# Conformer convolution: from four phases with two chunks on VectorE to eight phases with all chunks on TensorE

## The chip, the cores and the metric

One core of a Trainium2 chip. The metric is device microseconds of one launch, as the median of three runs.

## The reference

Two decoder layers on 512 tokens of 1024 channels, in float32. Each layer is a half-step SwiGLU feed-forward, a token mixer and a second half-step feed-forward, each between RMS norms and added to the residual. The mixer of layer 0 is sliding-window attention; that of layer 1 is the convolution module that the change is about:

```
a = h @ w_pw1 + b_pw1                       # 512 x 2048
u = a[:, :1024] * sigmoid(a[:, 1024:])
y = causal depthwise conv of u, width 31, one filter per channel, + b_dw
y = silu(layer_norm over the 1024 channels (y))
out = y @ w_pw2 + b_pw2
```

## The kernel before

Activations lie transposed, channels on the 128 partitions and 512 tokens along the row, so 1024 channels are 8 chunks. All dense products run on TensorE as three products each (high part by high part, high by low, low by high; L401 to L403). The weights come as one stream of slots of 128 x 1024 floats. SyncE loads slot n into a ring of four (`load`, L286), ScalarE copies its high part (L971) once TensorE has finished slot n - 4, VectorE subtracts to get the low part (`next_slot`, L1259), and TensorE multiplies it (`body`). VectorE takes the result from PSUM with the RMS factor (`scale_to`, L1292).

The first pointwise layer has 16 slots, two for each chunk: the value and the gate. When both are scaled, ScalarE takes the sigmoid (L1196) and VectorE makes u (`gate`, L1547 or L1553).

The depthwise convolution is done in two ways. Chunks 0 and 1 (`NAT = 2`) are done on VectorE, one tap at a time, each a multiply and add over 128 x 512 (`taps`, L1604 and L1608), spread by hand between the other instructions of the loop over chunks. The other six (`CONVS = 6`) are done on TensorE. The tokens of a chunk are put in `PH = 4` phases, token n*4 + q into phase q. u goes to DRAM and comes back with (channel, phase) on the partitions, 32 channels x 4 phases for each of 4 groups (`store_u` L306, `load_groups` L312). In that layout the 31 taps become `SHIFTS = 9` banded matrices per group, made on the host. One chunk is 2 pairs of groups x 9 shifts x 4 tiles of 64 x 64 = 72 matmuls of 128 columns in float32 (`convolve`, L857). The matrices, 2 of 576 KB a chunk, lie in five places (`MATS = 5`) and are loaded by SyncE (L302).

The norm over channels needs a mean over all of them. A mean over four early chunks is taken first (`sum_early`, L877) and subtracted from all; what is left of the mean and the sum of squares are added up by TensorE (L868, L891), and two broadcasts bring them to all partitions (`broadcast_phases`, L937). z goes through DRAM to the layout of channels again (L316, L320), is normalised (L1683, L1686), and the second pointwise layer starts (`four_slots`, L468 to L472).

All engines run orders written out by hand, tied by semaphores. TensorE's in this stage is: slots 4 and 5, slot 6, then for each of the first four chunks two slots and `convolve`, slot 15, the early mean, chunk 4 in two halves with the spread of the mean between them (L930), chunk 5 in two halves with sums between. VectorE's last split (slot 15) stands before its last gate.

Of the kernel before, what the change touches and what calls it, by code (L numbers as in the profile page):

```python
# [54 lines left out]
PH = 4  # L55
# [8 lines left out]
NAT = 2  # L64
CONVS = KD - NAT
EARLY = 4
# [32 lines left out]
def build_program(nc, stream, xT, cols_in, rope_c, rope_s, ident_in, ident_b_in, mask_in, mats_in, conv_in,  # L99
                  u_dram, z_dram, outT):  # L100
    ctx = ExitStack()
    with ctx:
# [3 lines left out]
        def sem(name):  # L106
# [37 lines left out]
        ug = al[:, 0:2 * GROUPS * (PAD + NT)].rearrange("p (i g n) -> p i g n", i=2, g=GROUPS)  # L144
        conv_c = sb("conv_consts", [P, P + CONVS * GROUPS + NAT * (CW + 1)])
        same_q, b_dw = conv_c[:, 0:P], conv_c[:, P:P + CONVS * GROUPS]
        at = P + CONVS * GROUPS
        w_nat = [[conv_c[:, at + c * CW + i:at + c * CW + i + 1] for i in range(CW)] for c in range(NAT)]
        at += NAT * CW
        b_nat = [conv_c[:, at + c:at + c + 1] for c in range(NAT)]  # L150
        at += NAT

        extra = sb("tap_matrix", [P, SHIFTS * P])
        spare = extra[:, 0:2 * T]
        swapped = [*(a_lo[:, k, :].bitcast(F32) for k in range(KD)), spare[:, 0:T], spare[:, T:2 * T]]
        MAT = 2 * SHIFTS * HALF
        extra2 = sb("tap_matrix2", [P, MAT])
        mats = [*(fv[:, i * MAT:(i + 1) * MAT] for i in range(3)), extra[:, :], extra2[:, :]]
        MATS = len(mats)

        kf = kT[:, :, :].rearrange("p a n -> p (a n)")
        zg = [z.rearrange("p (g n) -> p g n", g=GROUPS) for z in
              (kf[:, 0:T], kf[:, T:2 * T], rc[:, :], rs[:, :], U[:, 1, :], G[:, 1, :])]
        zsq_sum, *zsq = [z.rearrange("p (g n) -> p g n", g=GROUPS) for z in (G[:, 0, :], U[:, 0, :], ss[:, :])]
        m0 = sb("mean_early", [P, NT])
        dl, dl_sq, var = sb("mean_rest", [P, PH]), sb("mean_rest_sq", [P, PH]), sb("var", [P, PH])
        std = var
        early = sq[:, 0, :].rearrange("p (j n) -> p j n", j=EARLY)
        y = qT
        yv = y[:, :, :].rearrange("p a n -> p (a n)")  # L170
        u_nat = [yv[:, NAT * T + c * (CW - 1 + T):NAT * T + (c + 1) * (CW - 1 + T)] for c in range(NAT)]
        nat_acc = [y[:, KD - NAT + c, :] for c in range(NAT)]
        nat_sq, nat_sum = nat_acc, sq[:, 1, :]
# [6 lines left out]
        conv_out = [two_banks[i] for i in (3, 2, 3, 2, 3, 0)]  # L180
# [54 lines left out]
        s_ug = [sem(f"u_groups_loaded{i}") for i in range(2)]  # L235
# [5 lines left out]
        s_tap, s_m0bc, s_nat = sem("tap_added"), sem("early_mean_broadcast"), sem("direct_chunk_centred")  # L241
        s_nsq, s_nsum = sem("direct_chunk_squared"), sem("direct_chunks_added")
# [28 lines left out]
        def _(sp):  # L271
# [26 lines left out]
            def load_matrices(i):  # L298
                for k in range(MATS + PAIRS * (i - 1) if i else 0, min(MATS + PAIRS * i, PAIRS * CONVS)):
                    if i:  # L300
                        sp.wait_ge(s_cv, k - MATS + 1)
                    sp.dma_start(mats[k % MATS], mats_in[k // PAIRS, k % PAIRS, :, :]).then_inc(s_mats[k % MATS], 16)  # L302

            def store_u(i):
                sp.wait_ge(s_u, NAT + i + 1)
                sp.dma_start(u_dram[i, :, :], u[i % 2]).then_inc(s_ud[i % 2], 16)  # L306

            def load_groups(i):
                sp.wait_ge(s_ud[i % 2], 16 * (i // 2 + 1))
                if i >= 2:  # L310
                    sp.wait_ge(s_cv, PAIRS * (i - 1))
                sp.dma_start(ug[:, i % 2, :, PAD:], by_groups(u_dram, i)).then_inc(s_ug[i % 2], 16)  # L312
# [5 lines left out]
            def load_y(i):  # L318
                sp.wait_ge(s_zd[i % 4], 16 * (i // 4 + 1))
                sp.dma_start(y[:, NAT + i, :], z_dram[i, :, :]).then_inc(s_y[NAT + i], 16)  # L320
# [18 lines left out]
            sp.wait_ge(s_nat, NAT)  # L339
            for i in range(EARLY):  # L340
                load_y(i)
            store_z(4)
            sp.wait_ge(s_sqmm, 1)
            load_y(4)
            store_z(5)
            load_y(5)
            loads(conv_turn + PW1_SLOTS // RING, SLOTS // RING)
# [12 lines left out]
        def _(pool):  # L360
# [28 lines left out]
            for i in range(2):  # L389
                nc.gpsimd.memset(ug[:, i, :, 0:PAD], 0.0).then_inc(s_zeros, 1)  # L390
            for c in range(NAT):
                nc.gpsimd.memset(u_nat[c][:, 0:CW - 1], 0.0).then_inc(s_zeros, 1)
# [5 lines left out]
        def _(pe):  # L398
# [436 lines left out]
            def convolution(n0, sub):  # L835


                def convolve(j, halves=range(PAIRS)):

                    if 0 in halves:  # L840
                        pe.wait_ge(s_ug[j % 2], 16 * (j // 2 + 1))
                        if j == 0:
                            pe.wait_ge(s_zeros, 4)
                        if j == 1:
                            pe.wait_ge(s_rpre, sub + 1)
                        if j >= 2:
                            pe.wait_ge(s_zg, j - 1)
                        if j == CONVS - 1:
                            pe.wait_ge(s_evac, n0 + 14)
                    for i in halves:  # L850
                        k = PAIRS * j + i
                        pe.wait_ge(s_mats[k % MATS], 16 * (k // MATS + 1))
                        for m in range(SHIFTS):
                            for odd, rows, out in ((0, 0, 0), (0, 1, 1), (1, 0, 1), (1, 1, 0)):
# [4 lines left out]
                                                        ug[at, j % 2, 2 * i + odd, m:m + NT],  # L859
# [3 lines left out]
                def sum_groups(out, src, first, last):  # L863

                    for g in range(GROUPS):
                        for part in range(2):
                            to = slice(part * HALF, (part + 1) * HALF)
                            ins = nc.tensor.matmul(out[to, 0:PH], src[:, g, to], same_q[:, 0:PH],  # L868
                                                   start=(first and g == 0), stop=(last and g == GROUPS - 1),
                                                   skip_group_check=True)  # L870
                    return ins

                def sum_early():
                    pe.wait_ge(s_zg, EARLY)
# [6 lines left out]
                def sum_rest(j):  # L881
                    pe.wait_ge(s_zc, j + 1)
                    sum_groups(BCAST, zg[j], False, j == CONVS - 1).then_inc(s_dlmm, 1)

                def sum_direct(out, src, ready, first):

                    pe.wait_ge(s_nsum, ready)
                    for q in range(PH):
                        for part in range(2):
                            to = slice(part * HALF, (part + 1) * HALF)  # L890
                            ins = nc.tensor.matmul(out[to, q:q + 1], src[:, q * NT + to.start:q * NT + to.stop],  # L891
                                                   ones[:, 0:1], start=(first and q == 0), stop=False,
                                                   skip_group_check=True)
                    return ins

                def sum_squares(added):
                    if added:
                        pe.wait_ge(s_root, 3 * sub + 1)
                        sum_direct(STAT, nat_sq[0], 2, True)
                        pe.wait_ge(s_zsqadd, CONVS - 2)  # L900
                        sum_groups(STAT, zsq_sum, False, False)
                        return
                    pe.wait_ge(s_zsq, CONVS)
                    sum_groups(STAT, zsq[(CONVS - 1) % 2], False, True).then_inc(s_sqmm, 1)
# [22 lines left out]
            def spread_phases(out, v):  # L927

                for q in range(PH):
                    ins = nc.tensor.matmul(out[:, q * NT:(q + 1) * NT], ident[:, q:q + 1].broadcast_to([P, P]),  # L930
                                           v[:, :], start=True, stop=True)
                return ins

            def broadcast_phases(out, v):

                for q in range(PH):
                    ins = nc.tensor.matmul(out[:, q * NT:(q + 1) * NT], v[:, q:q + 1].broadcast_to([P, P]),  # L937
# [920 lines left out]
```

## Time and profile before

| | |
|---|---|
| median of three runs | 1828.2 us (1825.47 to 1830.34) |
| profiled execution | 1828.89 us, span 1827.1 us |
| TensorE busy in the span | 1808.8 us, 99% |
| VectorE busy in the span | 1020.5 us, 56% |
| slots 6 to 15 of the first pointwise layer and the convolution, to the first product of the second | 1304.1 to 1404.97 us |

The span is the time between the first and the last instruction of the profiled execution. A busy TensorE is one that has products in flight; they overlap, so the lengths of single products don't add up to a time, and the distances of their starts do.

### The profile page before, as it was taken

How to read it: one execution, taken by the hardware profiler on the slowest of the kernel's cores; microseconds unless marked ns; L12 is line 12 of the kernel's file. 1: busy time of each engine (PE TensorE's matmuls, PEld its weight loads, DVE VectorE, ACT ScalarE, POOL GpSimd, SP SyncE). 2: the span in 40 equal slices, each digit the busy share in tenths (PEclk: the TensorE clock that was granted, in tenths of full speed). 3: DMA queues.
4: the chain of work that ended last, by engine and by line, in shares of the span. 5: the costliest groups of instructions: out<-in, count | busy, mean ns of one | idle time of the engine just before them, and what ended most of it. 6: DMA issues, size and time to landing. Idle time of an engine off the chain costs nothing.

```text
span 1827.1 us, 26277 instructions
## 1 busy us (share of the span) xinstructions
PE 1808.8 (99%) x9934; PEld 1508.4 (83%) x9941; DVE 1020.5 (56%) x1484; ACT 644.1 (35%) x977; POOL 31.2 (2%) x60
## 2 busy tenths in 40 slices
PE   9999999999999999999999999999998999999999
PEld 7888888887698888888888888888887988888887
DVE  6534434589767434434774344347898774344345
ACT  5322313455744223222442232224414542222223
POOL 1000000022000000000000000000000000000000
PEclk9999999999999999999999999999998999999999
DMA  6333333422032333333333333333544333333331
GB/s 205 116 96 102 92 101 92 119 86 79 10 96 93 102 93 92 104 92 102 106 94 102 92 92 104 93 103 104 180 162 138 93 94 102 92 92 104 93 102 58
DMA packets 64078, 186.09 MB, mean 102 GB/s; under 512 B 7264, under 2 KB 19168, under 8 KB 64000
## 3 DMA queue, kind: packets, MB, share of 16 engines
q1 hardware_dynamic: 61824, 182.69, 32.7%
q0 software_dynamic: 1600, 1.52, 0.3%
q8 instruction: 55, 0.90, 0.2%
q10 hardware_dynamic: 576, 0.79, 0.1%
q14 instruction: 23, 0.19, 0.0%
HBM read 179.08 MB, written 5.24 MB: 101 GB/s over the span
## 4 chain that ended last, share of the span: by engine, by line
PE 92%; DVE 5%; issue 1%; ACT 1%; DMA 0%; ACTq 0%; SPq 0%; DVEq 0%
PE bank L401 27%; PE bank L402 27%; PE bank L403 27%; PE bank L494 4%; DVE qT L1608 2%; PE bank L499 2%; DVE w_lo L1259 1%; PE bank L762 1%; PE bank L794 1%; PE bank L738 1%; PE bank L428 1%; PE bank L777 0%; PE bank L420 0%; PE bank L857 0%; PE bank L441 0%
## 5 line engine op out<-in xcount | busy, mean ns | idle before, releaser
L1259 DVE TENSOR_TENSOR w_lo<-w_raw,w_hi 128x1024 fp32r<-128x1024 f32 x302 | 369.2, 1225 | 417.2 <-ACT w_hi L971 406.6
L401 PE MATMUL bank<-x_hi,w_hi 128*128 128x512 f32 x1432 | 558.9, 390 | 0.0
L402 PE MATMUL bank<-x_lo,w_hi 128*128 128x512 f32 x1432 | 557.2, 389 | 0.0
L403 PE MATMUL bank<-x_hi,w_lo 128*128 128x512 f32 x1432 | 557.2, 389 | 0.0
L971 ACT ACTIVATE w_hi<-w_raw 128x1024 fp32r<-128x1024 f32 x302 | 317.1, 1054 | 559.9 <-PE bank L403 547.4
L401 PE MATMUL bank<-a_hi,w_hi 128*128 128x512 f32 (+1 forms) x894 | 331.5, 371 | 1.1 <-issue 1.1
L402 PE MATMUL bank<-a_lo,w_hi 128*128 128x512 f32 (+1 forms) x894 | 329.6, 369 | 0.0
L403 PE MATMUL bank<-a_hi,w_lo 128*128 128x512 f32 (+1 forms) x894 | 329.5, 369 | 0.0
L403 PEld LDWEIGHTS bank<-x_hi,w_lo 128*128 128x128 f32 x1432 | 268.8, 188 | 56.3
L401 PEld LDWEIGHTS bank<-x_hi,w_hi 128*128 128x128 f32 x1432 | 268.8, 188 | 56.2 <-issue 0.7
L402 PEld LDWEIGHTS bank<-x_lo,w_hi 128*128 128x128 f32 x1432 | 268.8, 188 | 55.2
L401 PEld LDWEIGHTS bank<-a_hi,w_hi 128*128 128x128 f32 x894 | 168.4, 188 | 30.9 <-issue 1.6
L403 PEld LDWEIGHTS bank<-a_hi,w_lo 128*128 128x128 f32 x894 | 168.4, 188 | 28.2
L402 PEld LDWEIGHTS bank<-a_lo,w_hi 128*128 128x128 f32 x894 | 168.5, 188 | 28.1
L1292 DVE TENSOR_TENSOR up_tmp<-bank,r_pre 128x512 f32<-128x512 f32 x96 | 66.2, 690 | 183.7 <-PE bank L403 182.3
L1009 ACT ACTIVATE a_hi<-up_tmp 128x512 f32 (+1 forms) x88 | 55.6, 632 | 267.2 <-DVE up_tmp L1302 267.2
L1007 ACT ACTIVATE gate_tmp<-gate_tmp 128x512 f32<-128x512 f32 x88 | 55.7, 632 | 158.3 <-DVE gate_tmp L1292 158.2
L1304 DVE TENSOR_TENSOR a_lo<-up_tmp,a_hi 128x512 f32 (+1 forms) x88 | 60.9, 692 | 79.9 <-ACT a_hi L1009 79.9
L1292 DVE TENSOR_TENSOR gate_tmp<-bank,r_pre 128x512 f32<-128x512 f32 x106 | 72.3, 683 | 7.1 <-ACT r_pre L995 6.9
L1302 DVE TENSOR_TENSOR up_tmp<-up_tmp,gate_tmp 128x512 f32<-128x512 f32 x88 | 60.9, 692 | 13.7 <-ACT gate_tmp L1007 3.3
L980 ACT ACTIVATE x_hi<-h_resid,cols 128x256 fp32r<-128x256 f32 (+1 forms) x88 | 46.5, 528 | 44.3 <-DVE h_resid L1378 41.6
L1314 DVE TENSOR_TENSOR f_out<-bank,f_out 128x512 f32 (+2 forms) x73 | 45.0, 620 | 25.1 <-PE bank L403 25.0
(206 smaller groups left out, 1322.1 us busy)
## 6 DMA issues: line engine op xcount, KB each, us to landing
w_raw<-stream SPq DMA_DIRECT2D x312, 512.0 KB, 3.6
f_out<-mats_in SPq DMA_DIRECT2D x8, 576.0 KB, 5.6
tap_matrix<-mats_in SPq DMA_DIRECT2D x4, 576.0 KB, 7.3
h_resid<-xT SPq DMA_DIRECT2D x8, 256.0 KB, 6.0
qT<-stream SPq DMA_DIRECT2D x8, 256.0 KB, 6.2
u_scratch<-V SPq DMA_DIRECT2D x6, 256.0 KB, 2.2
a_lo<-u_scratch SPq DMA_DIRECT2D x6, 256.0 KB, 2.7
qT<-z_scratch SPq DMA_DIRECT2D x6, 256.0 KB, 3.6
```

The source lines that it names most:

```text
L401: nc.tensor.matmul(out, lw[0], lx[0], start=first, stop=False)
L402: nc.tensor.matmul(out, lw[0], lx[1], start=False, stop=False)
L403: return nc.tensor.matmul(out, lw[1], lx[0], start=False, stop=last)
L494: nc.tensor.matmul(bank[FIRST_BANKS[s]][:, tok], w[KD * s + k][part], x_hi[:, k, tok], start=(k == 0 and tok == A and part == 0), stop=Fal ...
L971: nc.scalar.activation(w_hi[:, s, :], raw[:, s, :], ACT.Copy).then_inc(s_hi, 1)
L980: nc.scalar.activation(x_hi[:, k, tok], h[:, k, tok], ACT.Copy, scale=col("pre", sub * KD + k)).then_inc(done, 1)
L1007: nc.scalar.activation(g, g, ACT.Silu).then_inc(s_act, 1)
L1009: nc.scalar.activation(a_hi[:, chunk, :], U[:, (s // 2) % 2, :], ACT.Copy).then_inc(s_ahi, 1)
L1259: nc.vector.tensor_tensor(w_lo[:, s, :], raw[:, s, :], w_hi[:, s, :].bitcast(F32), ALU.subtract).then_inc(s_lo, 1)
L1292: nc.vector.tensor_tensor(dst, out[:, :], r_pre[:, :], ALU.mult).then_inc(s_evac, 1)
L1302: nc.vector.tensor_tensor(U[:, p, :], U[:, p, :], G[:, p, :], ALU.mult).then_inc(s_prod, 1)
L1304: nc.vector.tensor_tensor(a_lo[:, chunk, :], U[:, p, :], a_hi[:, chunk, :].bitcast(F32), ALU.subtract).then_inc(s_a, 1)
```

## The change

The convolution runs in eight phases. A chunk then has 8 groups of 16 channels x 8 phases of 64 tokens, 5 shifts, and 4 pairs x 5 shifts x 4 tiles = 80 matmuls of 64 columns. All eight chunks go this way, and the taps on VectorE with all that belongs to them are gone. The matrices are 4 of 320 KB a chunk, in 14 places: eight are loaded by SyncE ahead of the slots of the third feed-forward block, six after it, and the other 18 by ScalarE, in sets, as places come free. u of seven chunks has room at once. The early mean is over three chunks. The last gate stands ahead of the last split of a weight slot, z of the last chunk is stored last, and statistics and broadcasts have eight phases on 64 partitions.

```diff
-PH = 4
+PH = 8
-NAT = 2
-CONVS = KD - NAT
-EARLY = 4
+CONVS = KD
+EARLY = 3
...
             conv_turn = (PW1 + 2 * RING) // RING
-            loads(2, conv_turn)
+            loads(2, FFN2 // RING + 1)
+            first_matrices(FREE_MATS)
+            loads(FFN2 // RING + 1, conv_turn)
             for j in range(KD):
                 n = PW1 + 2 * RING + 2 * j
                 load(n, n % RING)
-                if j >= RING:
-                    load_matrices(j - RING + 1)
-                load(n + 1, (n + 1) % RING)
+                if j < KD - 1:
+                    load(n + 1, (n + 1) % RING)
                 if j == 0:
                     sp.wait_ge(s_root, 3 * 4 + 1)
-                    load_matrices(0)
-                if j >= NAT:
-                    store_u(j - NAT)
-                    load_groups(j - NAT)
-            load_matrices(CONVS - 1)
-            for i in range(EARLY):
+                    first_matrices(F_MATS)
+                store_u(j)
+                load_groups(j)
+            load(n + 1, (n + 1) % RING)
+            for i in range(EARLY + 1):
                 store_z(i)
...
                 first_body(n0, sub)
-                body(n0 + 6, 2)
                 for i in range(EARLY):
-                    for n in range(2 * i + 7, 2 * i + 9):
+                    for n in range(2 * i + 6, 2 * i + 8):
                         body(n0 + n, n % RING)
                     convolve(i)
-                body(n0 + 15, 3)
+                body(n0 + 12, 0)
                 sum_early()
-                convolve(4, range(0, 1))
+                body(n0 + 13, 1)
+                convolve(EARLY)
+                for n in range(14, 16):
+                    body(n0 + n, n % RING)
+                for i in range(EARLY + 1, CONVS - 1):
+                    convolve(i)
                 pe.wait_ge(s_m0, 1)
-                spread_phases(BCAST, m0).then_inc(s_m0bc, 1)
-                convolve(4, range(1, 2))
-                convolve(5, range(0, 1))
-                pe.wait_ge(s_nat, NAT)
-                sum_direct(BCAST, nat_sum, 1, True).then_inc(s_dlmm, 1)
-                sum_rest(4)
-                convolve(5, range(1, 2))
-                sum_squares(True)
-                sum_rest(5)
-                sum_squares(False)
+                pe.wait_ge(s_rest, 2)
+                sum_groups(BCAST, rest, True, False)
+                convolve(CONVS - 1)
+                sum_centred(6)
+                pe.wait_ge(s_root, 3 * sub + 1)
+                pe.wait_ge(s_zsqadd, CONVS - 2)
+                sum_groups(STAT, zsq_sum, True, False)
+                sum_centred(7).then_inc(s_dlmm, 1)
+                pe.wait_ge(s_zsq, CONVS)
+                sum_groups(STAT, zsq[(CONVS - 1) % 2], False, True).then_inc(s_sqmm, 1)
...
+                def load_matrices(i, count=PAIRS):
+                    for k in range(MATS + PAIRS * i, MATS + PAIRS * i + count):
+                        act.wait_ge(s_cv, k - MATS + 1)
+                        act.dma_start(mats[k % MATS], mats_in[k // PAIRS, k % PAIRS, :, :]
+                                      ).then_inc(s_mats[k % MATS], 16)
...
                         scale_to((U, G)[e][:, j % 2, :], bank[FIRST_BANKS[n - n0] if n < n0 + RING else n % RING], n, 5)
+                        if (j, e) == (KD - 2, 0):
+                            dve.wait_ge(s_m0mm, 1)
...
                     gate(j)
-                    if 2 <= j < KD - 1:
-                        k = taps(k, 3 if j == 2 else 4)
+                    if EARLY <= j < 2 * EARLY:
+                        biased(j - EARLY)
+                        add_early(j - EARLY)
+                next_slot(n, n % RING)
                 centred(4)
```

## Rows read from the trace of the kernel before

**Rows 1.** The page: busy time of engines, and the span in 40 slices.
```profile
PE 1808.8 (99%) x9934; PEld 1508.4 (83%) x9941; DVE 1020.5 (56%) x1484; ACT 644.1 (35%) x977; POOL 31.2 (2%) x60
...
PEclk9999999999999999999999999999998999999999
```

**Rows 2.** The chain of waits at the convolution's end: start us, us, what.
```profile
1375.22 3.97 DVE qT L1608 x6
...
1384.56 2.88 DMA u_scratch<-V
...
1387.46 2.92 DMA a_lo<-u_scratch
...
1404.97 0.50 PE bank L468
```

**Rows 3.** TensorE's timeline in that stage: start us, us, line, output<-inputs, count, idle before.
```profile
1299.23 0.39 PE L401 MATMUL bank<-x_hi,w_hi 128*128 128x512 f32 x1
...
1318.95 0.39 PE L401 MATMUL bank<-x_hi,w_hi 128*128 128x512 f32 x1
...
1320.40 4.16 PE L857 MATMUL bank<-a_lo,f_out 64*64 64x128 f32 x144
...
1335.64 2.20 PE L857 MATMUL bank<-a_lo,f_out 64*64 64x128 f32 x72
...
1379.85 1.89 PE L877 MATMUL bank<-sq_tmp,conv_consts 128*128 128x128 f32 x8 [3.85 <-DVE rope_sin L1583]
1381.66 3.24 PE L857 MATMUL bank<-a_lo,tap_matrix 64*64 64x128 f32 x72
...
1390.42 3.86 PE L857 MATMUL bank<-a_lo,f_out 64*64 64x128 f32 x72 [2.30 <-DMA a_lo<-u_scratch]
...
1399.55 1.16 PE L937 MATMUL bank<-ident,mean_rest 128*128 128x128 f32 x8
1400.71 1.91 PE L937 MATMUL bank<-ident,var 128*128 128x128 f32 x8
```

**Rows 4.** Stretches: busy us and instructions of PE, PEld, DVE, ACT, POOL; granted clock; DMA share; GB/s.
```profile
1380.40:1383.85 3.45, 3.45 (x46) 2.98 (x48) 2.66 (x4) 1.19 (x2) 0.00 (x0) 0.51 0.25 52
1390.69:1394.10 3.41, 3.41 (x72) 3.25 (x64) 3.20 (x6) 1.26 (x2) 0.00 (x0) 0.50 1.07 330
...
1397.44:1404.97 7.53, 7.14 (x86) 5.34 (x87) 4.20 (x11) 3.91 (x7) 0.00 (x0) 0.77 0.37 100
```

**Rows 5.** VectorE's groups from 1304.1 to 1405: count, busy us, mean ns, idle before.
```profile
L1608 DVE SCALAR_TENSOR_TENSOR qT<-qT,conv_consts 128x512 f32<-128x512 f32 x60 | 40.5, 744 | 0.0
L1259 DVE TENSOR_TENSOR w_lo<-w_raw,w_hi 128x1024 fp32r<-128x1024 f32 x12 | 14.6, 1216 | 0.2 <-ACT w_hi L971 0.2
L1553 DVE SCALAR_TENSOR_TENSOR V<-up_tmp,cols,gate_tmp 128x512 f32<-128x512 f32 x6 | 6.9, 1156 | 4.7 <-ACT gate_tmp L1196 4.7
...
L1292 DVE TENSOR_TENSOR gate_tmp<-bank,r_pre 128x512 f32<-128x512 f32 x6 | 4.1, 681 | 0.0
L1640 DVE TENSOR_REDUCE sq_tmp<-kT 128x128 f32<-128x512 f32 x2 | 2.2, 1076 | 0.1
...
L1583 DVE TENSOR_TENSOR kT<-bank,conv_consts 128x512 f32<-128x512 f32 x2 | 1.4, 688 | 0.0
```

**Rows 6.** Products in flight on TensorE in two short stretches of chunk 0's convolution.
```profile
1320.60:1320.65 0.05, 0.05 (x8) 1.00 0.23 82
1320.66:1320.71 0.05, 0.05 (x12) 1.00 0.60 246
```

**Rows 7.** TensorE's timeline: small sums on two tiles, and the attention's transposes.
```profile
492.95 0.71 PE L777 MATMUL bank<-ident,f_out 64*128 64x64 f32 x16
...
1398.99 0.64 PE L868 MATMUL bank<-conv_consts,sum_sq 128*64 128x4 f32 x16
```

**Rows 8.** The DMA view, 1290 to 1404: count, KB each, median us to landing.
```profile
tap_matrix<-mats_in SPq DMA_DIRECT2D x4, 576.0 KB, 7.3
```

**Rows 9.** SyncE's queue: the weight loads of slots 10 to 13.
```profile
1297.16 11.12 SPq L286 DMA_DIRECT2D w_raw<-stream  x4
```

More of the change, by code:

```diff
@@ L148, in build_program @@
[L148 to L154, printed above, removed]
+        spare = sb("spare", [P, 2 * T])[:, :]
         swapped = [*(a_lo[:, k, :].bitcast(F32) for k in range(KD)), spare[:, 0:T], spare[:, T:2 * T]]
         MAT = 2 * SHIFTS * HALF
-        extra2 = sb("tap_matrix2", [P, MAT])
@@ L158, in build_program @@
-        mats = [*(fv[:, i * MAT:(i + 1) * MAT] for i in range(3)), extra[:, :], extra2[:, :]]
-        MATS = len(mats)
+        more = sb("tap_matrices", [P, 2 * MAT])[:, :]
         kf = kT[:, :, :].rearrange("p a n -> p (a n)")
+        y = qT
+        yv = y[:, :, :].rearrange("p a n -> p (a n)")
+        Y_MATS = 5
         zg = [z.rearrange("p (g n) -> p g n", g=GROUPS) for z in
-              (kf[:, 0:T], kf[:, T:2 * T], rc[:, :], rs[:, :], U[:, 1, :], G[:, 1, :])]
+              (kf[:, 0:T], kf[:, T:2 * T], rc[:, :], rs[:, :], yv[:, Y_MATS * MAT:Y_MATS * MAT + T],
+               U[:, 1, :], u[0], G[:, 1, :])]
@@ L171, in build_program @@
-        u_nat = [yv[:, NAT * T + c * (CW - 1 + T):NAT * T + (c + 1) * (CW - 1 + T)] for c in range(NAT)]
-        nat_acc = [y[:, KD - NAT + c, :] for c in range(NAT)]
-        nat_sq, nat_sum = nat_acc, sq[:, 1, :]
+        early = sq[:, 0, :].rearrange("p (j n) -> p j n", n=NT)
+        rest = sq[:, 1, :].rearrange("p (g n) -> p g n", g=GROUPS)
+        mats = [room[:, i * MAT:(i + 1) * MAT]
+                for room, first, count in ((spare, 0, 1), (more, 0, 2), (fv, 0, 1), (yv, 0, Y_MATS), (fv, 1, 5))
+                for i in range(first, first + count)]
@@ L174, in build_program @@
+        MATS = len(mats)
+        F_MATS = 3, 9, 10, 11, 12, 13
+        FREE_MATS = [i for i in range(MATS) if i not in F_MATS]
         first_raw = qT[:, :, :].rearrange("p a n -> p (a n)").rearrange("p (s n) -> p s n", s=RING)
@@ L234, in build_program @@
         s_ud = [sem(f"u_in_dram{i}") for i in range(2)]
-        s_ug = [sem(f"u_groups_loaded{i}") for i in range(2)]
+        s_ug = [sem(f"u_groups_loaded{i}") for i in range(CONVS)]
         s_zd = [sem(f"z_in_dram{i}") for i in range(4)]
@@ L296, in by_groups, with first_matrices @@
                 return dram[j, :, :].rearrange("(g c) (q n) -> (c q) g n", g=GROUPS, q=PH)
[L298 to L302, printed above, removed]
+            def first_matrices(which):
+                for k in which:
+                    sp.dma_start(mats[k], mats_in[k // PAIRS, k % PAIRS, :, :]).then_inc(s_mats[k], 16)
             def store_u(i):
-                sp.wait_ge(s_u, NAT + i + 1)
+                sp.wait_ge(s_u, i + 1)
                 sp.dma_start(u_dram[i, :, :], u[i % 2]).then_inc(s_ud[i % 2], 16)
@@ L865, in sum_groups, with sum_centred @@
                     for g in range(GROUPS):
[L866 to L870, printed above, removed]
-                    return ins
+                        ins = nc.tensor.matmul(out[0:NT, 0:PH], src[:, g, :], same_q[:, 0:PH],
+                                               start=(first and g == 0), stop=(last and g == GROUPS - 1),
+                                               skip_group_check=True)
+                    return ins
+                def sum_centred(j):
+                    pe.wait_ge(s_zc, j + 1)
+                    return sum_groups(BCAST, zg[j], False, j == CONVS - 1)
                 def sum_early():
-                    pe.wait_ge(s_zg, EARLY)
+                    pe.wait_ge(s_rpre, sub + 1)
                     for j in range(EARLY):
@@ L879, in sum_early @@
                     last.then_inc(s_m0mm, 1)
[L881 to L894, printed above, removed]
@@ L1843 @@
     b_groups = np.broadcast_to(b_dw[0][order].reshape(KD * GROUPS, GC, 1), (KD * GROUPS, GC, PH)).reshape(KD * GROUPS, P).T
-    direct = (*(w_dw.reshape(CW, D)[:, c * P:(c + 1) * P].T for c in range(NAT)), cols(b_dw[0])[:, :NAT])
     bf = ml_dtypes.bfloat16
```

212 lines of the change are left out of this document (89 added, 123 removed).

## The prediction

> **What bounds the kernel now.** I read the page first. TensorE is busy through nearly the whole span, at full clock in all slices but one, so only work or waits of TensorE inside the convolution can move the time; the one slice at 0.8 of the clock lies there [rows 1]. The chain of waits over that stretch says what sets the pace at its end: VectorE with its taps (L1608), then the gate, then two transfers, then TensorE again from 1390.42 [rows 2]. So for the changed stretch I take TensorE's own timeline [rows 3] and VectorE's groups [rows 5], and split TensorE's 100.9 us between the start of slot 6 and the first product of the second pointwise layer.
>
> A slot of the first pointwise layer is 8 blocks of 0.680 us (29 blocks between 1299.23 and 1318.95), 5.44 us; slot 6 starts three slots ahead of the first convolution, at 1320.40 - 16.3 = 1304.1. From one convolution to the next it is 15.24 us [rows 3]: two slots (10.88) and a chunk of 4.36. A chunk is 144 products (72 matmuls, each recorded as two); less the length of the last one they start 27.2 ns apart ((4.16 - 0.27) / 143), 3.92 us, and 0.44 is spent at the turns from one kind of product to the other. Ten slots (54.4) and four chunks (17.4) bring TensorE to 1375.9. Then it waits 3.9 us for VectorE's z of chunk 3; sums the early mean (1.8); convolves chunk 4 in halves, the first in 3.2, with a spread of the mean between them; waits 2.3 for the last u to come back from DRAM; and takes 7.0 for chunk 5 with sums between its halves, to 1397.44. The first product of the next layer starts 7.53 us later. The two halves that take 3.2 and 3.8 instead of 2.1 lie in stretches with the clock at 0.50 to 0.51, the lower level of 1.2 GHz, behind the 3.9 us of idling [rows 4].
>
> **The change, part by part.** *Taps off VectorE.* 62 instructions go, 60 of which are 40.5 us; with them go six operations on the direct chunks. In their place come two more z (0.69 each), three additions and small ones [rows 5]. In the steady part VectorE then has two splits, two scalings, a wait for the sigmoid, a gate, a bias and a reduction for each two slots: 2 x 1.22 + 2 x 0.68 + 4.7 / 6 + 1.16 + 0.69 + 1.08 = 7.5 us beside at least 13 us on TensorE. So it is never late there: each z is ready some 10 us before the next convolution wants its banks, and the 3.9 us wait, the clock loss behind it and the spread go.
>
> *All chunks on TensorE, eight phases.* A chunk becomes 4 pairs x 5 shifts x 4 tiles = 80 matmuls, 160 products, of 64 columns instead of 128, and there are eight chunks. All depends on what a product of 64x64 weights and 64 columns costs, which no row shows. In the conv of now four products start within 0.06 us (8 in flight from 1320.60 to 1320.65, 12 from 1320.66 to 1320.71) [rows 6]: four tiles run side by side, each with a new product every 4 x 27.2 = 109 ns, that is 0.85 ns for each of 128 columns. 64 columns would be 54 ns. The smallest products of the trace, 64 columns of weights and 1 or 4 moving ones on two tiles, start (0.64 - 0.20) / 15 = 29.3 ns apart [rows 7], 58.6 ns for each tile, which is then about what a load of 64 columns costs a tile. If that 58.6 belongs to the tile, four tiles give 14.7 ns a product and a chunk costs 2.34 us. If instead 27 to 29 ns belongs to the stream of instructions, whatever the tile, a chunk costs 4.35 to 4.7. The transposes, on two tiles as well, show 32.6 ns ((0.71 - 0.22) / 15) [rows 7]. I take the tile's reading, because four starts within 0.06 us speak against a spacing by instruction, and because the conv of now gets the same 27 ns from four tiles at 109 that the small sums get from two at 58.6. Bounds: 13.3 (columns alone) and 32.6 ns.
>
> The Trainium skill has a rule against this: TensorE: Matmul & The Clock Gate, section Back-to-back issue gap, gives 1 to 64 columns the same gap of about 60 cycles, a floor of some 25 ns from start to start. By that rule a chunk would cost 4.0 us, and eight such chunks more than the six of now. The Trainium skill's page TensorEngine Tiling (Array Packing), section Tiling Modes, says on the other hand that different tiles execute weight loads and matmuls in parallel; that part the trace bears out with its four starts within 0.06 us.
>
> *TensorE up to slot 15.* Ten slots 54.4, four chunks at 2.34 + 0.44 = 11.1, early mean 0.7 (six products instead of eight, at full clock): 66.2, so slot 15 ends at 1370.3, where it now ends at 1375.9. Chunks 4 to 6 follow without a slot between: 0.2 + 7.0, and the sum of the rest 0.5, to 1378.0.
>
> *Last gate ahead of the last split.* Now a split stands before the gate. Scaling of the last slot (0.68), the wait for its sigmoid (4.7 / 6), gate (1.16), the way to DRAM (2.88) and back (2.92) are 8.4 us with 0.1 for the steps between, 8.5 [rows 2, 5]. With scaling at 1370.5 the last chunk can begin at 1379.0. The groups are read in runs of 256 B instead of 512 B, for which no row exists; I add 0.5 (bounds 0 and, at twice the 2.92, 2.9). So chunk 7 starts at 1379.5, 1.5 us after TensorE is free. This chain of transfers, not TensorE, is what is late next, and it is all that is left of the old waits. It ends at 1381.9.
>
> *Tap matrices on ScalarE's queue.* 32 matrices of 320 KB replace 12 of 576 KB: 3.3 MB more. Eight go out before the third feed-forward block's first slots, six at its end, 18 from ScalarE. At the boundary the weight ring has slack: a slot's load stands some 20 us ahead of its split, and 2.6 MB at the 330 GB/s that a stretch here shows [rows 4] take 8 us. In the conv ScalarE issues each set of four after a split, for places free since the convolution before, and is busy for 35% of the span [rows 1]. The last two go out at about 1373.5; 576 KB ones took 7.3 us to land [rows 8], so they land by 1380.8 at worst, where the third pair starts at 1380.7. Nothing, or 0.5 us.
>
> *SyncE's queue.* The first weight load of the stretch is now queued behind the first u and its reading back: 1303.4 instead of 1297.16 [rows 9]. It lands at 1307 and is wanted after slot 6, at 1309.5: nothing. z of chunk 7 is stored last and read back by about 1391; its channel is normalised eighth, some 13 us after the first. Nothing.
>
> *The tail.* The same steps from the last convolution on, 7.53 us [rows 2, 3], but each broadcast of eight phases is 16 products with 128 columns of weights instead of 8, at up to 0.124 ((1.16 - 0.29) / 7). The mean's starts at 1399.55 and then ends at 1401.4, the deviation's 1.9 later, at 1403.3 instead of 1402.6 [rows 3]: +0.7. The clock may fall again in the 1.5 us gap or in the tail; today's tail has it at 0.77 [rows 4]. I give 0.3 for it, with 0 and 3 as bounds.
>
> Sum: 1381.9 + 0.3 + 7.53 + 0.7 = 1390.4, against 1404.97: 14.6 us less. From there on nothing changes. The profiled execution took 1828.9 us around a span of 1827.1, 0.7 over the median of the three runs; 1828.9 - 14.6 - 0.7 = 1813.6, so 1814.
>
> **Rivals.** *The floor belongs to the instructions (27.2 ns).* Slot 15 ends at 1304.1 + 54.4 + 4 x 4.79 + 0.7 = 1378.4, the last four chunks take 18.1, to 1396.5, and the tail 8.2: 1404.7, 0.3 us less than now. The waits are gone and the eight chunks have eaten them. At the 29.3 ns of the small sums it is 2.7 us more. Time 1828 to 1831, no change. For it: no run of products in these rows averages less than 27.2 ns. This is what the rule of the Trainium skill quoted above amounts to; with its own 25 ns the time would be 1825.
>
> *In between, 20 ns*, if loads of four tiles partly share a port: chunks of 3.2. Slot 15 at 1373.8, last chunk to 1387.2, tail to 1395.4: 9.5 less, 1819.
>
> *Slower.* The 64x64 products keep to the transposes' 32.6 ns [rows 7]: 1280 products x 5.4 ns = 6.9 more than at 27.2, so 6.6 slower, 1835. It decides from 31.7 ns on. Against it: those have twice the columns of weights.
>
> **Chances.** Tile's floor 0.66, between 0.07, instruction's floor 0.21, slower 0.06. 0.3% of this kernel is 5.5 us, about what a measurement of it can tell from no change. The first two are faster, 0.73; same 0.21; slower 0.06. The likeliest case alone has 1810 to 1819: 13.3 ns and no loss of clock at the lower end (two to three less), slow pieces in the transfers and a low clock at the upper. The whole range goes from 1810 to 1829 and leaves out the upper half of the instruction's floor and the slower case.
>
> **What would show it.** The convolution's line with 1280 products; a run of 160 in about 2.5 us (4.4 if I am wrong); from one convolution to the next about 13.7 us instead of 15.24; no wait of TensorE for VectorE before the early mean; a wait of 1 to 2 us for the transfer of u before the last chunk; VectorE's L1608 gone and its share down from 56%; the full clock up to slot 15. If the period stays near 15.7, the floor was the instruction's and the prediction is wrong there. If the period is right and the end isn't, look at the matrices from ScalarE's queue and at the 256 B runs.

## The result and the profile after

The changed kernel takes 1833.3 us (median of 8 runs, 1831.9 to 1838.4) where the one before takes 1828.0 on the same chip (8 runs): ratio 1.0032, 95% interval 1.0023 to 1.0042. It is 5.3 us slower by the medians. I had forecast 1814, within 1810 to 1829.

The page of the profiled execution (1832.03 us, span 1830.2), to set beside [rows 1]:

```profile
PE 1810.6 (99%) x10347; PEld 1510.9 (83%) x10347; DVE 982.8 (54%) x1425; ACT 643.8 (35%) x977; POOL 31.1 (2%) x63
...
PEclk9999999999999999999999999999997999999999
...
q8 instruction: 58, 0.95, 0.2%
```

VectorE lost its taps, as the change says. The slice of the convolution has a clock of 0.7 instead of 0.8. The last line I had passed over in both pages: a queue of its own brings instructions, 0.95 MB in 58 transfers, that is 16 KB each.

TensorE's timeline answers to [rows 3] (start us, us, line, output<-inputs, count, idle before):

```profile
1327.47 2.56 PE L856 MATMUL bank<-a_lo,qT 64*64 64x64 f32 x160
1341.07 0.81 PE L856 MATMUL bank<-a_lo,qT 64*64 64x64 f32 x40
1341.70 1.91 PE L856 MATMUL bank<-a_lo,f_out 64*64 64x64 f32 x114
1345.00 0.34 PE L856 MATMUL bank<-a_lo,f_out 64*64 64x64 f32 x6 [1.40 <-issue]
1350.85 0.78 PE L878 MATMUL bank<-sq_tmp,conv_consts 128*128 128x64 f32 x6
```

A whole chunk is 160 products in 2.56 us; less the length of the last, 0.22, they start 14.7 ns apart, as forecast. From the first convolution (1313.87) to the second and third it is 13.6 us. The early mean no longer waits for VectorE. But chunk 2 stops after 154 products (40 + 114) for 1.40 us, and the row names no releaser but "issue": nothing that the profile knows held TensorE.

The chain of waits from there on answers to [rows 2] (start us, us, what):

```profile
1370.74 3.66 PE bank L856 x240
1374.40 1.84 issue
1376.24 2.09 PE bank L856 x124
1378.34 1.75 issue
1380.09 1.86 PE bank L856 x112
1381.95 0.97 PE bank L865 x15
1382.92 3.25 issue
1386.18 0.17 PE bank L865
1386.35 3.37 PE bank L856 x127
1389.71 1.39 issue
1391.10 0.73 PE bank L856 x33
1391.84 6.20 PE bank L865 x64
1398.04 7.02 PE bank L910 x32
```

The last gate and the transfers of the last u are not in this chain at all; [rows 2] had them. The products run out three times ahead of the last chunk and once inside it. Count them between two stops: 124 in the chain (the timeline has all 128 there), then 112 + 15 = 127, then 1 + 127 = 128. Each product goes with one weight load (the page has 10347 of either), so each stop comes after about 256 instructions, and 16 KB for 256 instructions are 64 bytes each. The Trainium skill's page Advanced Engine Details and Errata, section ISA Cache, has the same size: a line of 16 KB holds 256 instructions, and there are only two lines (it also gives TensorE's cache as 128 KB, which would hold more). The trace agrees with the 256; how many lines there are no run here settles, and the page has no price for a line. The DMA view puts the transfer of such a piece ahead of the end of a stop. Of three stretches of the third stop, 1382.92 to 1383.88, to 1384.85 and to 1386.20, it is in the second (queue, transfers, MB, share of time):

```profile
q1 hardware_dynamic: 935, 0.24, 106.5%
q8 instruction: 1, 0.02, 6.0%
```

TensorE goes on 1.3 us after it. The same holds for the other four stops of this trace: each ends 1.4 to 1.7 us after a piece has moved. From one restart to the next a piece takes 3.85, 6.09 and 4.92 us, and 128 products at 14.7 ns use one up in 1.9.

Stretches with the granted clock answer to [rows 4] (us; busy us and instructions of PE, PEld, DVE, ACT, POOL; clock; DMA share; GB/s):

```profile
1370.74:1374.40 3.66, 3.66 (x241) 3.56 (x241) 2.87 (x4) 2.83 (x3) 0.00 (x0) 1.00 0.93 333
...
1385.85:1389.26 3.41, 3.08 (x113) 2.98 (x115) 0.00 (x0) 0.00 (x0) 0.00 (x0) 0.50 0.93 245
...
1392.67:1407.41 14.74, 14.74 (x90) 12.91 (x88) 3.51 (x10) 3.91 (x7) 0.00 (x0) 0.50 0.40 110
```

Behind the stops the clock is at its lower level, 1.2 GHz, for 3.4 us and then for the 14.7 us up to the first product of the next layer (and 2.3 us beyond it, 17.1 in all). From the start of slot 6 (1302.99) to that product (1407.41) it is 104.4 us; before it was 100.9, and I had forecast 86.3.

### The profile page after: what moved, and what is told of

It is laid out like the page before. It is cut to its first block, busy times and chain, and to the rows that moved or that the text cites. A ratio compares the mean times of both kernels' runs of the same rounds, so it can differ in the third digit from the quotient of the medians.

```text
span 1830.2 us, 27076 instructions
## 1 busy us (share of the span) xinstructions
PE 1810.6 (99%) x10347; PEld 1510.9 (83%) x10347; DVE 982.8 (54%) x1425; ACT 643.8 (35%) x977; POOL 31.1 (2%) x63
## 4 chain that ended last, share of the span: by engine, by line
PE 97%; DVE 1%; issue 1%; ACT 0%; ACTq 0%
PE bank L397 28%; PE bank L399 28%; PE bank L398 28%; PE bank L490 4%; PE bank L495 2%; PE bank L856 1%; PE bank L790 1%; PE bank L734 1%; PE bank L758 1%; PE bank L424 1%; PE bank L416 0%; PE bank L773 0%; PE bank L865 0%; PE bank L910 0%; PE bank L437 0%
## 5 line engine op out<-in xcount | busy, mean ns | idle before, releaser
L1278 DVE TENSOR_TENSOR gate_tmp<-bank,r_pre 128x512 f32<-128x512 f32 x106 | 72.4, 684 | 7.1 <-ACT r_pre L968 6.9
```

The costliest lines, as they stand in the source:

```text
L1278: nc.vector.tensor_tensor(dst, out[:, :], r_pre[:, :], ALU.mult).then_inc(s_evac, 1)
```

## The experiments

The theories: **F**, TensorE outruns the supply of its instructions wherever many cheap products stand in a row. **U**, the late last chunk is due to the transfers around the last u and z. **C**, a TensorE that idles falls to the lower clock, and that makes the last chunk, the small sums and the broadcasts dear. All kernels are edits of the changed one. "Stage" is the time from the first product of the convolution to the first product of the next layer in the profiled execution: 93.5 us in the changed kernel. In the kernel before, counted from the same point, 10.9 us after the start of slot 6, it is 90.0, of which 10.2 at the lower clock. "Last chunk begins after" counts from the first product of the convolution, and "lower clock" is the time at 1.2 GHz within the stage, both in us of the profiled execution. Each ratio is to the kernel before on the same chip, with a 95% interval, from 4 to 12 runs of a version.

| kernel | median us | ratio to before, interval | stage | last chunk begins after | lower clock |
|---|---|---|---|---|---|
| the change | 1833.3 | 1.0032, 1.0023 to 1.0042 | 93.5 | 72.4 | 18.2 |
| double_mid | 1834.9 | 1.0045, 1.0028 to 1.0062 | 95.8 | 77.2 | 18.9 |
| double_late | 1837.0 | 1.0052, 1.0035 to 1.0069 | 97.5 | 79.5 | 17.8 |
| few_shifts | 1826.9 | 0.9996, 0.9986 to 1.0006 | 88.6 | 67.2 | 20.9 |
| early_z | 1834.1 | 1.0032, 1.0019 to 1.0044 | 95.7 | 73.6 | 23.2 |
| no_mats | 1831.9 | 1.0019, 1.0009 to 1.0030 | 93.1 | 70.5 | 21.4 |
| filled | 1833.7 | 1.0031, 1.0020 to 1.0043 | 91.9 | 73.5 | 16.6 |
| interleave | 1829.5 | 1.0009, 0.9999 to 1.0018 | 96.3 | 73.9 | 24.5 |
| interleave_warm | 1827.6 | 1.0000, 0.9990 to 1.0009 | 89.4 | 72.9 | 10.1 |
| few_warm | 1829.0 | 1.0008, 0.9998 to 1.0018 | 90.3 | 75.2 | 15.0 |
| inter_short | 1830.5 | 1.0018, 1.0009 to 1.0027 | 93.1 | 69.7 | 17.6 |
| inter_tail | 1832.4 | 1.0023, 1.0011 to 1.0034 | 98.9 | 72.0 | 25.7 |
| warm_tail | 1828.5 | 1.0003, 0.9994 to 1.0012 | 93.1 | 71.2 | 16.6 |

A profile is one execution, and these kernels spread more than the one before: interleave from 1825.4 to 1834.9 (its profiled execution took 1834.9), inter_tail from 1825.5 to 1837.2 (profiled: 1837.2). So the medians decide on times, and the profiles on what happens in which order.

**A chunk's products twice.** In the middle (chunk 1), and at the end (chunk 5).

```diff
-                        for m in range(SHIFTS):
+                        for m in (*range(SHIFTS), *range(SHIFTS if j == 5 else 0)):
```

> The products of chunk 1, which lie between slots 9 and 10, are issued twice (320 instead of 160; the result is the same). Theory F (TensorE outruns the supply of its own instructions: in the changed kernel's trace it idles four times at the end of the convolution, 1.4 to 3.3 us, each time 128 products, that is 256 instructions, after the last, and each idling ends 1.4 to 1.7 us after a 16 KB instruction transfer): 128 products between slots are supplied ahead while a slot runs, so most of the extra ones cost 14.7 ns, 2.4 us, and at most one idling of 1.5 us is added: 5.8 + 2.4 to 3.9, ratio to the kernel before 1.0045 to 1.0055. Theory U (the end of the convolution waits for the last u and its DRAM trip, and the rest is the lower clock): slot 15 ends 2.4 us later and everything with it, 1.0045.

> The products of chunk 5, which follow chunk 4 with no slot between, are issued twice (same result). Theory F: each 128 products there take the 3.85 to 6.1 us from one idling to the next and not 1.9, so 160 more take 4.8 to 7.6 us, and there is one more idling: ratio 1.006 to 1.0075. Theory U: TensorE only waits there for the last u, which lands at about 1380.4, 5.9 us before the last chunk begins, so 2.4 us more are hidden: ratio 1.003 as without them.

double_mid: 236 products in 3.65 us, a stop of 1.73, then 84 more, in the middle of the layer, with the same "issue" as the releaser. double_late, the chain of waits:

```profile
1371.38 3.66 PE bank L856 x240
1375.04 1.84 issue
1376.88 2.09 PE bank L856 x125
1378.97 1.63 issue
1380.61 2.10 PE bank L856 x125
1382.70 3.45 issue
1386.15 2.09 PE bank L856 x128
1388.25 3.55 issue
```

The reader is to see the counts: 240, and then one stop for every 128 products, whatever chunk they belong to. 160 products more moved the last chunk by 7.0 us (79.5 - 72.4), not by 2.3. That is F, and no wait for data gives this pattern.

The times say less. double_late costs 3.7 us against the change, less than the 4.8 to 7.6 that F had: in its profile the stage is only 4.0 longer, since the last chunk, late as it is, runs without a stop. double_mid costs 1.6, and the intervals of the two overlap, so that late products are dearer than early ones is shown by the traces and not by the times.

**Fewer products.** Leaves out three of five shifts in chunks 4 to 6.

```diff
-                        for m in range(SHIFTS):
+                        for m in ((0, PAD) if j in (4, 5, 6) else range(SHIFTS)):
```

> Leaves out three of the five shifts of chunks 4, 5 and 6: 64 products each instead of 160, 288 fewer in all. Theory F: two idlings less before the last chunk; it starts when the last u has landed, at about 1381 instead of 1386.3, at full clock, and the tail goes back from 15.6 us towards 8.2 to 10: 10 to 13 us less than the changed kernel, ratio to before 0.996 to 0.998. Theory U: what sets the start of the last chunk is not TensorE's own work, so it starts within 0.5 us of 1386.3 and the ratio stays at 1.003.

```profile
1373.33 4.51 DMA u_scratch<-V
...
1377.85 2.85 DMA a_lo<-u_scratch
...
1380.74 4.32 PE bank L856 x159
1385.06 1.55 issue
1386.62 0.27 PE bank L856
1386.88 5.89 PE bank L865 x64
1392.77 7.02 PE bank L910 x32
```

Now the transfers of the last u are in the chain, as the prediction had them, and the last chunk begins at 1380.74, 5.3 us earlier than in the change. U falls: it had the last chunk where it was. For F this run alone says little, since 288 products fewer are 4.2 us less work even at 14.7 ns. And the clock did not recover as I had expected: TensorE idled 4.3 us for VectorE's last z, ran at half clock from 1377.8, and the tail kept its 13 us (5.89 + 7.02). So the supply is only a part of the loss.

**z of chunks 0 to 2 stored ahead of the last u.**

```diff
+                if j == KD - 1:
+                    for i in range(EARLY):
+                        store_z(i)
                 store_u(j)
...
-            for i in range(EARLY + 1):
-                store_z(i)
+            store_z(EARLY)
```

> The stores of z of chunks 0 to 2 stand ahead of the last u's store on SyncE's queue (they are centred by 1356) instead of behind its reading back. Theory F with contention (the third idling, 3.25 us, is long because the 16 KB of instructions stand behind z stores in pieces of 256 B): it shrinks to 1.5 to 2, 1 to 3 us less than the changed kernel, ratio 1.0015 to 1.0025. If instructions have their way free of other transfers: 1.003, and the third idling stays over 3 us.

The third stop stayed (3.25 us), and the time is that of the change. This does not clear the transfers of z, though. With its stores out of the way, SyncE issues the reading back of z earlier, from 1382.48, and between the restart at 1382.28 and the piece at 1385.94 the DMA engines still move 282 GB/s. What the piece waits behind stays open here.

**No late matrices.** Leaves out the loads of the last six tap matrices and TensorE's waits for them (not shown in the cut).

```diff
-                        if e == 0 and j >= RING:
+                        if e == 0 and RING <= j < KD - 1:
                             load_matrices(j - RING)
...
-                load_matrices(KD - RING, PAIRS * CONVS - MATS - PAIRS * (KD - RING))
```

> Leaves out the loads of the last six tap matrices (2 MB between 1366 and 1378), so chunks 6 and 7 use older ones. Theory F with contention (the third piece of 256 instructions came late, 3.8 us instead of 1.05 after TensorE resumed, because the DMA engines were full of matrices and z): the idlings of 1.84, 1.75 and 3.25 us shrink, the third to under 2, the last chunk starts 2 us earlier, 1831. If the supply has its own pace, nothing moves: 1833.

The stops are 0.89, 1.48 and 1.61 us instead of 1.84, 1.75 and 3.25, and the last chunk begins 1.9 us earlier, as F with contention said; inside the last chunk one of 2.38 us gives part of it back (the change has 1.39 there). In the traces data traffic stretches the supply, and without these loads TensorE still stops; the median is 1.4 us lower, which the intervals can't tell from no change. Note two things more. The store of the last u took 2.0 us here (issued 1374.71, read back from 1376.73) and 3.8 in the change (1373.50, 1377.30). And the clock fell at 1385.9 as in the change, though none of these three stops was longer than 1.61.

**Work that fills the stops.** Four products of 512 columns behind chunk 4 and behind chunk 5.

```diff
                 for i in range(EARLY + 1, CONVS - 1):
                     convolve(i)
+                    if i < 6:
+                        keep_warm(4, out=4)
```

> The changed kernel with four products of 512 columns (0.85 us, eight instructions) added after chunk 4 and again after chunk 5, into a free bank; nothing is left out. It has 1.7 us more work in the stretch that sets the end. Theory F (TensorE's idlings there are waits for instructions, 3.85 us or more a piece of 256 whatever it computes): the added products fill idling time, the idlings of 1.84, 1.75 and 3.25 us shrink by about what is added, and the last chunk starts within 0.5 us of where it did (72.4 us after the first convolution): 1833, perhaps 1 less where the clock stays up. If the idlings are something else (a wait for a bank or for data), all comes 1.7 us later: 1835.

1.7 us of work more cost 0.4 us by the medians, less than the measurement can tell. In the profiled execution, the fastest of six (1829.35), the stops ahead of the small sum are 1.08 and 0.39 us instead of 1.84 and 1.75, but the third was still 3.05, and the last chunk began 1.1 us later (73.5), not the 0.5 that I had allowed. By the medians most of the added work was free. The counts tell more: the first stop comes after 160 + 4 + 76 = 240 products and the next after 84 + 4 + 40 = 128, with the four big products counted like all others. The stops go by the number of instructions, whatever these compute.

**Chunk 4 between slots 14 and 15.**

```diff
                 for n in range(14, 16):
                     body(n0 + n, n % RING)
-                for i in range(EARLY + 1, CONVS - 1):
-                    convolve(i)
+                    convolve(n - 10)
+                convolve(6)
```

On VectorE `centred(3)` moves from slot 14's place to right behind the gate of chunk 6.

> Chunk 4 is convolved between slots 14 and 15, so that after slot 15 two chunks (5 and 6, 320 products) stand in a row instead of three (480); VectorE centres chunk 3 right after the gate of chunk 6. Nothing is left out. Slot 15 ends 2.3 us later (about 1373 instead of 1370.6), so the last u is back at 1382.8 instead of 1380.4. Theory F (TensorE gets its instructions in pieces of 256, and a long run of cheap products outruns the supply): slot 14 and slot 15 refill it on either side of chunk 4, the two chunks cost 4.7 us and one idling of 1.5 to 2, so they are done by 1380; the last chunk starts when its u is there, 1382.8 to 1383.5 instead of 1386.3, and the first product of the next layer comes 3 us earlier, 1404: 1830.3 us. Theory U (the last chunk is late because of the transfers behind the last u): it starts 2.3 us later than in the changed kernel, 1388.6, and the time is 1835.

The median fell by 3.8 us, to 1829.5 where F had 1830.3 and U 1835 (the ratio's interval lies apart from that of the change). The profiled execution does not show it: it is the slowest of ten, chunk 2 alone stands still for over 3 us in it, and behind slot 15 there are stops of 2.00 us in chunk 6 and 2.24 in the last chunk. The last u is in its chain of waits again.

**Big products while the last u is awaited.** 16 in interleave_warm and 4 in inter_short, both on top of interleave, and 28 in few_warm on top of few_shifts.

```diff
                 sum_groups(BCAST, rest, True, False)
+                keep_warm(16, out=4)
                 convolve(CONVS - 1)
```

> As interleave, with 16 products of 512 columns (0.21 us each at full clock, 3.4 us in all) into a free bank ahead of the last chunk, so that TensorE does not idle while it waits for the last u. Nothing is left out. Theory C (an idling TensorE loses its clock, and the half clock is what makes the last chunk and the small sums dear): no half clock between 1376 and 1402, the last chunk in 2.3 to 2.5 us, the 64 small-sum products in 3.8 instead of 6.2, the 32 broadcast ones in 3.5 to 4 instead of 7.0: 6 us earlier than interleave, first product of the next layer near 1398, 1824 us. If the clock falls for another reason (the cheap products themselves), the half clock stays and the time is within 1 us of interleave.

> interleave_warm with 4 products ahead of the last chunk in place of 16, since there they ended 2.6 us after the last u could have been back (by the changed kernel, 9.8 us from the end of slot 15 to its landing). Nothing is left out. Theory C with F: the last chunk starts 2 to 2.6 us earlier, 70.3 us after the first convolution instead of 72.9, the clock stays full through the last chunk, first product 87.2 us after the first convolution instead of 89.4: 1825.5. If 4 are too few to keep the clock up, the tail takes 5 us more and it ends like interleave, 1829.

> Leaves out three of the five shifts of chunks 4, 5 and 6, as few_shifts does, and puts 28 products of 512 columns (6.0 us at full clock) ahead of the last chunk. In few_shifts TensorE idled there for 4.5 us and ran at half clock afterwards. Theory C: with the idling filled the clock stays full, the last chunk still starts near 1380.7, takes 2.3 us (perhaps plus one idling of 1.5 to 2 for instructions) instead of 4.1, and the small sums and broadcasts 7.5 instead of 13 us: first product at 1395 to 1397 instead of 1402.2, 1820 to 1822 us. If the half clock stays, the time is that of few_shifts, 1827, or more.

The chain of waits of interleave_warm, and the stretches around the fall of its clock:

```profile
1383.27 0.52 issue
1383.79 0.17 PE bank L865
1383.95 3.56 PE bank L408 x16
1387.51 1.78 PE bank L856 x111
1389.30 0.28 issue
1389.58 0.97 PE bank L856 x49
1390.54 4.10 PE bank L865 x64
1394.64 7.02 PE bank L911 x32
```

```profile
1374.98:1393.90 18.92, 15.97 (x572) 13.31 (x571) 10.89 (x17) 5.68 (x8) 0.00 (x0) 1.00 0.74 200
1393.90:1404.01 10.11, 10.11 (x47) 8.28 (x45) 3.19 (x8) 3.28 (x6) 0.00 (x0) 0.50 0.80 198
```

The last chunk runs at full clock with a stop of only 0.28 us, and the small sums take 4.1 instead of 6.2; the broadcasts stay at 7.0, since the clock falls at 1393.9, 0.7 us ahead of the end of the sums. The time, 1827.6, is 1.9 below interleave, which the overlapping intervals can hardly tell, and not the 6 that C had. Now inter_short:

```profile
1382.28 0.24 issue
1382.53 0.17 PE bank L865
1382.70 0.97 PE bank L408 x4
1383.66 2.00 PE bank L856 x123
1385.67 3.71 issue
1389.38 1.33 PE bank L856 x34
```

With 4 instead of 16 the last chunk begins 3.1 us earlier (69.7 after the first convolution against 72.9), stops 3.7 us for instructions, and ends no earlier: its last product starts after 76.5 us against 75.7. Count again from one stop to the next: 1 + 16 + 111 = 128 there, 1 + 4 + 123 = 128 here. With 12 big products fewer, 12 more of the chunk come ahead of the same stop. This chunk too began at full clock (1.00 up to 1389.4, the end of its stop), so what the 12 further products gave was not warmth but time for the supply: 16 of them last 3.56 us, as long as some 240 of the chunk's. The time is 1830.5, where C with F had 1825.5. few_warm, against few_shifts, is the test of the clock in the last chunk: it came back to 1.00 while the 28 ran (at half clock at first, so they took 8.98 us and not 6.0), the last chunk took 2.49 us without any stop and the sums 3.83, and it fell again in the broadcasts. As a time it missed: I had expected 1820 to 1822, and it is 1829.0, 2.0 above few_shifts, because the 28 pushed the last chunk from 67.2 to 75.2 us.

**Big products in the tail.** inter_tail is inter_short with the 5 and 3 big products below; warm_tail is interleave_warm with them, and with 14 instead of 16 ahead of the last chunk.

```diff
                 sum_groups(STAT, zsq_sum, True, False)
+                keep_warm(5, out=0)
                 sum_centred(7).then_inc(s_dlmm, 1)
...
             def layer_norm():

+                keep_warm(3, out=0)
                 pe.wait_ge(s_dl, 1)
```

> inter_short with 5 products of 512 columns in the middle of the last small sums and 3 ahead of the two broadcasts, 1.7 us of added work at full clock. Nothing is left out. In interleave_warm the clock fell to half 3.4 us into the small sums, and the 32 broadcast products took 215 ns each. Theory C (small products leave TensorE's array so idle that it loses the clock): with the big products among them the clock stays full, the broadcasts take 107 ns each, 3.4 us less, and the products ahead of the next layer 1.1 less; net 2.5 to 3 us earlier than inter_short: 1823. If the clock falls all the same, it is 1.7 us later than inter_short.

> interleave_warm with 14 products of 512 columns ahead of the last chunk (16 there), and the 5 and 3 of inter_tail among the last small sums and ahead of the broadcasts. Nothing is left out. In inter_tail the clock had already fallen in a 3.6 us idling inside the last chunk, so its tail said nothing on theory C; here the 14 products leave the supply of instructions its time first. Theory C: full clock from the last chunk through the broadcasts, these take 107 ns each instead of 215, first product 86.5 to 87.5 us after the first convolution instead of 89.4: 1825. If small products lose the clock whatever stands among them, it falls within the tail all the same, and the first product comes 1.3 us later than in interleave_warm: 1829.

Both missed. In inter_tail the clock had fallen before the tail, and the added products ran at half clock as well. In warm_tail it was full up to 1390.2, behind a stop of 0.63 us in the last chunk, and fell among the small sums all the same; the time is 0.9 us above interleave_warm, by the ratios 0.03%, which is nothing that these runs can tell.

## Why the prediction was wrong

The step that failed is the one in "TensorE up to slot 15" by which chunks 4 to 6 follow "without a slot between: 0.2 + 7.0", with the transfers of the last u as all that is left of the waits. In place of 7.7 us, the three chunks and the small sum behind them took 15.6 (1370.7 to 1386.3), because TensorE ran out of instructions in them. With it fell two terms of "The tail": the same steps in 7.53 us, and 0.3 us for the clock. Counted from the start of slot 6, the first product of the next layer came 18.1 us later than forecast:

* *Price of a product.* Right: 14.7 ns, a run of 160 in 2.56 us, a period of 13.6 us. The rival that gave the floor to the instructions (27.2 ns) is refuted where instructions are at hand. The 25 ns from start to start that the Trainium skill gives in TensorE: Matmul & The Clock Gate, section Back-to-back issue gap, does not hold for four tiles side by side: the trace has 14.7 on average.
* *Taps off VectorE.* Right: no wait of TensorE for z before the early mean, and VectorE's share is 54%. Slot 15 was done 1.3 us later than forecast, by the stop of 1.40 in chunk 2.
* *Three chunks in a row.* Wrong. The start of the last chunk was forecast 75.4 us after slot 6's and came at 83.3 (1386.30 - 1302.99), 7.9 later: 1.3 brought along, 6.84 from the stops of 1.84, 1.75 and 3.25, 1.3 more where the sum of the rest and the run-out of the last products at each stop took longer, less the 1.5 us wait for u that these hide. I asked for each chunk what data it waits for and never how fast instructions come. From 1376.24 to 1391.10 three pieces, 384 products, took 14.9 us, 38.7 ns a product. That is dearer than the rivals of 27.2 and 32.6 ns, by another mechanism. The kernel before never shows it: at 27.2 ns a piece lasts 3.5 us, its longest run is 144 products, and slots follow.
* *The last chunk.* 2.4 us forecast, 5.5 measured: a stop of 1.39, and half clock in part (0.57 over its first 127 products).
* *The tail.* 8.5 us forecast, 15.6 measured (1391.77 to 1407.41), 7.1 more. "The same steps" was wrong by itself: 64 products of small sums now stand on one tile of 64 columns instead of two, and take 3.83 us at full clock (few_warm) where the 29.3 ns of [rows 7] make it 1.9 for 64: 1.9 us more. The rest is the clock: sums at 6.20 instead of 3.83, broadcasts 7.02 instead of the 3.7 forecast, which is about half of it: their own size was right (in few_warm the first of them, at full clock, start 0.11 us apart, and those after the fall 0.21), their clock was not.
* *Queues.* "Nothing, or 0.5 us" for the matrices from ScalarE's queue was too little. The store of the last u was forecast at the 2.88 us of [rows 2]; it took 3.8 in the change, 4.51 in few_shifts, and 2.0 without the last matrices. In the change the stops hide this. Where they are gone, in few_shifts, the last chunk still begins 78.1 us after slot 6 and not 75.4: 1.6 of the 2.7 are the store, and most of the rest is the stop in chunk 2. So this term would have been wrong by itself. By the trace of no_mats the matrices also stretched the supply of instructions. The reading back in pieces of 256 B took 2.85 in few_shifts: the 0.5 added for it wasn't needed.

The range missed because both ways to be slower that I had weighed were prices of one product. What I left open: what makes the clock fall in the tail. For the last chunk C is borne out by one profile each of two pairs: it ran at full clock where the wait ahead of it was filled (few_warm, interleave_warm), and at half, at once or from its middle on, where TensorE had idled (few_shifts, interleave). How much idling it takes is not shown, and in the tail the clock fell in each version, with and without big products among the small ones. Nor is it shown why a piece takes 3.85 us in one place and 6.09 in another; by one profile the matrices are a part of it.

No version beats the kernel before. interleave_warm, which has all eight chunks on TensorE and leaves nothing out, ties with it and is 5.7 us below the change by the medians (ratios to before 1.0000 and 1.0032).

## What to carry to other kernels

When an edit makes products cheaper and more numerous, multiply the instructions as well as the time: a run of matmuls with a weight load each is limited by what brings the instructions, here 128 products in 3.85 to 6.1 us once the first 240 are used up. Put long slots between the bursts, so that the supply catches up; that made it better here and not whole, since chunk 2, with two slots ahead of it, stopped 1.4 us in the change and over 3 in interleave. A wait of a few us ahead of the stage that ends the path costs more than itself, since what follows may run at half clock.

## What the runs showed of the hardware

* Instructions come to TensorE in pieces of 16 KB, 256 instructions. In a burst TensorE does up to 240 products on what it has (154 in chunk 2), then stops after each 127 or 128, big products counted like small ones; it goes on 1.3 to 1.7 us after a piece has moved.
* Such a stop stands in the chain of waits as "issue" on TensorE of over 1 us, with no releaser. Without the last matrices' loads the three stops of 6.84 us in all were 3.98.
* 64x64x64 products on four tiles start 14.7 ns apart; small sums with 64 columns of weights on one tile 60 ns (3.83 us for 64, in few_warm).
* Behind 4.3 us of idling the clock was at its lower level for 6.8 us (few_shifts); behind stops of 0.89, 1.48 and 1.61 us it fell as well (no_mats). The 32 broadcast products took 7.0 us at it, and 6.4 in few_warm, where it fell among them.
